# A decoder step on one core: the crossed plain products of three chunks left out, VectorE writing their result across the partition halves, and the first round slots laid out anew

## The reference

```python
def step(S, inp):
    r_t, w_t, k_t, v_t, kk_t, b_t = inp
    sk = jnp.einsum('bhvk,bhk->bhv', S, kk_t)
    S = S * w_t[:, :, None, :] - sk[..., None] * b_t[:, :, None, :] + v_t[..., None] * k_t[:, :, None, :]
    return S, jnp.einsum('bhvk,bhk->bhv', S, r_t)

def _layer(x, pos, s_wkv, s_ret, s_shift, p):
    h = _rmsnorm(x, p['norm_mix_pre'])
    z = h @ p['w_in']
    ya, s_wkv, s_shift = _rwkv7_branch(za, s_wkv, s_shift, ...)
    yb, s_ret = _retention_branch(zb, pos, s_ret, p['gn_b_gain'], p['gn_b_bias'])
    m = jax.nn.sigmoid(ga) * (ya @ p['w_out_a']) + jax.nn.sigmoid(gb) * (yb @ p['w_out_b'])
    x = x + _rmsnorm(m @ p['w_o'], p['norm_mix_post'])
    f = (jax.nn.silu(h @ p['w_ffn_gate']) * (h @ p['w_ffn_up'])) @ p['w_ffn_down']
```

## Time and profile before

| | |
|---|---|
| median of 3 runs | 1286.19 us (1283.54 to 1286.68) |
| the profiled execution | 1286.61 us |
| its span, first to last instruction | 1284.4 us |
| mean granted TensorE clock | 0.988 |
| the rounds of layer 0 | 109.45 to 160.76 us |
| the rounds of layer 1 | 740.29 to 792.47 us |

### The profile page before, as it was taken

One profiled execution on the slowest core, in us unless ns is written; L12 is line 12 of the kernel. 1 busy time (PEld: TensorE's weight loads), 2 busy tenths in 40 slices (PEclk: granted clock), 3 DMA queues, 4 the chain that ended last, 5 costly groups with the idle time before them and its releaser, 6 DMA issues.

```text
span 1284.4 us, 27898 instructions
## 1 busy us (share of the span) xinstructions
PE 1223.7 (95%) x12056; PEld 1159.6 (90%) x12056; DVE 859.4 (67%) x1476; ACT 558.1 (43%) x849; POOL 141.3 (11%) x160
## 2 busy tenths in 40 slices
PE   6999899999998999999999998999999989999996
PEld 5999787998998999999898987889889989999996
DVE  4887558888776666653388954688878566666433
ACT  4553345444435433344454544355453453333432
POOL 0004463100000000000000071900100000000000
PEclk9999999999998999999999999999999989999998
DMA  6433134644453545444434424264354435444441
GB/s 212 143 117 117 53 120 152 228 135 145 139 165 115 185 140 159 148 147 150 147 98 131 123 80 110 87 224 148 131 173 126 155 97 164 148 148 149 148 149 71
DMA packets 51177, 179.12 MB, mean 139 GB/s; under 512 B 6256, under 2 KB 7024, under 8 KB 49776
## 3 DMA queue, kind: packets, MB, share of 16 engines
q1 hardware_dynamic: 42576, 153.77, 38.1%
q10 hardware_dynamic: 8480, 23.58, 5.3%
HBM read 166.18 MB, written 8.53 MB: 136 GB/s over the span
## 4 chain that ended last, share of the span: by engine, by line
PE 82%; DVE 10%; ACT 4%; issue 3%; DMA 1%; ACTq 0%; SPq 0%; DVEq 0%
PE dense L1362 51%; PE core L1362 31%; DVE w_lo L890 3%; ACT w_hi L591 2%; DVE x L939 1%; DVE y_out L937 1%; DMA ret_s<-ret_t 1%; DVE ret_t L1288 1%; ACT L579 0%; DMA x<-x_t 0%; DVE bonus L1008 0%; DVE tmp L994 0%; ACT sq_pair L811 0%; DVE bonus L1004 0%; DVE s_ga L1160 0%
## 5 line engine op out<-in xcount | busy, mean ns | idle before, releaser
L890 DVE TENSOR_TENSOR w_lo<-w_raw,w_hi 128x1024 fp32r<-128x1024 f32 x282 | 352.8, 1253 | 222.0 <-ACT w_hi L591 220.8
L591 ACT ACTIVATE w_hi<-w_raw 128x1024 fp32r<-128x1024 f32 x282 | 297.8, 1057 | 446.6 <-PE dense L1362 300.0
L1362 PE MATMUL dense<-h_hi,w_hi 128*128 128x320 f32 x1296 | 416.8, 322 | 22.9 <-DVE h_lo L894 11.4
L1362 PE MATMUL dense<-h_lo,w_hi 128*128 128x320 f32 x1296 | 404.1, 312 | 0.0
L1362 PE MATMUL dense<-h_hi,w_lo 128*128 128x320 f32 x1296 | 404.0, 312 | 0.0
L1362 PEld LDWEIGHTS dense<-h_hi,w_hi 128*128 128x128 f32 x1296 | 246.9, 190 | 43.0 <-issue 35.0
L1362 PEld LDWEIGHTS dense<-h_lo,w_hi 128*128 128x128 f32 x1296 | 247.1, 191 | 1.4 <-issue 0.2
L1362 PEld LDWEIGHTS dense<-h_hi,w_lo 128*128 128x128 f32 x1296 | 246.7, 190 | 0.0
L1362 PE MATMUL core<-h_hi,w_hi 128*128 128x320 f32 x416 | 129.3, 311 | 0.0
L1362 PE MATMUL core<-h_hi,w_lo 128*128 128x320 f32 x416 | 128.9, 310 | 0.0
L1362 PE MATMUL core<-h_lo,w_hi 128*128 128x320 f32 x416 | 128.9, 310 | 0.0
(11 more groups left out here) (299 smaller groups left out, 1982.6 us busy)
## 6 DMA issues: line engine op xcount, KB each, us to landing
w_raw<-wts SPq DMA_DIRECT2D x282, 512.0 KB, 3.5
ret_t<-ret_t ACTq DMA_DIRECT2D x16, 256.0 KB, 3.7
ret_s<-ret_t ACTq DMA_DIRECT2D x16, 256.0 KB, 2.4
ret_rest<-ret_d ACTq DMA_DIRECT2D x2, 1536.0 KB, 8.6
qk_rot<-qk_raw SPq DMA_DIRECT2D x8, 320.0 KB, 6.2
dmask<-rconst ACTq DMA_DIRECT2D x2, 1152.0 KB, 5.6
s_st<-wkv_st ACTq DMA_DIRECT2D x2, 1024.0 KB, 5.0
wkv_s<-s_st ACTq DMA_DIRECT2D x2, 1024.0 KB, 4.2
```

The costliest lines, as they stand in the source:

```text
L591: act.activation(w_hi[n % RING][:, :], w_raw[n % RING][:, :], ACT.Copy).then_inc(hi_ready.sem, 1)
L890: dve.tensor_tensor(w_lo[r][:, :], w_raw[r][:, :], w_hi[r][:, :].bitcast(F32), ALU.subtract).then_inc(low_made.sem, 1)
L1362: return pe.matmul(out, lhsT, rhs, start=start, stop=stop)
```

## The change

Four things change, in both layers:

1. The jobs `mx1`, `mx2`, `mx3` are gone. For chunks 1 to 3, ACT copies the plain product into `m_sq` as before, and DVE then reads the same bank and writes the masked beginning of `x_sq` to the other half of the partitions, by two operations on 64 partitions each. It waits for the job and for ACT's copy first.
2. PE frees such a bank only when both have been there.
3. The first twelve slots become eleven, with `vt0`, `vt1` and `vt2` among them; slots 13 to 48 become 12 to 47, with `e14` and `d33` alone in theirs.
4. PIECE_AT, LOW_AT and MASKS follow. The pieces have the same sizes; POOL takes the four `xt` first, then the four `x`, and the levels' masks of chunk 0 after those of chunks 1 to 3.

```diff
-ROUNDS = ("vt0", "mt0 mx1", "mt1 mx2", "mt2 mx3", "mt3 kt0", "m0 kt1", "m1 kt2", "m2 kt3", "m3 e01", "mt4 e02", "e00 e03",
-          "m4 kt4", "tb0 dt01", "d01 tk0", "dt00 dt02", "d00 dt03", "d02 e11", "d03 tk1", "e10 e12", "e04 dt11", "dt10 e13",
+ROUNDS = ("mt1 kt0", "mt2 kt1", "mt3 kt2", "mt0 kt3", "m1 vt0", "m2 vt1", "m3 e01", "m0 e02", "mt4 e03", "e00 kt4",
+          "m4 vt2", "tb0 dt01", "d01 tk0", "dt00 dt02", "d00 dt03", "d02 e11", "d03 tk1", "e10 e12", "e04 dt11", "dt10 e13",
           "d10 dt12", "d11 tk2", "d12 dt13", "d13 e21", "e20 e22", "dt04 tk3", "d04 e23", "dt20 dt21", "d20 dt22", "d21 dt23",
-          "d22 tk4", "d23 e31", "e30 e32", "e14 vt1", "dt30 e33", "d30 dt31", "d31 dt32", "d32 dt33", "d33 vt2", "e40 e41",
+          "d22 tk4", "d23 e31", "e30 e32", "e14", "dt30 e33", "d30 dt31", "d31 dt32", "d32 dt33", "d33", "e40 e41",
           "dt14 e42", "tb1 vt3", "dt40 e43", "tb2 dt41", "tb3 dt42", "tb4 vt4", "dt43")
-PIECE_AT = {at: (n // 3, THIRDS[n % 3]) for n, at in enumerate((2, 5, 8, 12, 16, 20, 24, 28, 32, 37, 42, 48))}
-LOW_AT = {10: 1, 18: 2, 30: 3, 42: 4}
+PIECE_AT = {at: (n // 3, THIRDS[n % 3]) for n, at in enumerate((2, 5, 8, 11, 15, 19, 23, 27, 31, 36, 41, 47))}
+LOW_AT = {9: 1, 17: 2, 29: 3, 41: 4}
-MASKS = ("xt0", "x1", "xt1", "x2", "xt2", "x3", "xt3", "x0", "p10", "p20", "p11", "p21", "p12", "p22", "p13", "p23", "xt4", "x4",
+MASKS = ("xt1", "xt2", "xt3", "xt0", "x1", "x2", "x3", "x0", "p11", "p21", "p12", "p22", "p13", "p23", "p10", "p20", "xt4", "x4",
-PARTS = {"mt": ("xt", "mrb"), "m": ("x", "m"), "mx": ("x",)}
-V_OPS = [(part, lv, s) for name, lv, s in JOBS if not on_act((name, lv, s)) for part in PARTS.get(name, (name,))]
+PARTS = {"mt": ("xt", "mrb"), "m": ("x", "m")}
+def parts_of(job):
+    if on_act(job):
+        return ("x",) if job[0] == "m" else ()
+    return PARTS.get(job[0], (job[0],))
+V_OPS = [(part, job[1], job[2]) for job in JOBS for part in parts_of(job)]
...
-                    elif name in ("m", "mx"):
+                    elif name == "m" and s in FLIP:
+                        dve.wait_ge(*round_a(layer, A_AT[job]))
+                        for half in range(2):
+                            here, there = slice(C * half, C * half + C), slice(C - C * half, 2 * C - C * half)
+                            ins = dve.tensor_tensor(pairs(x_sq, s, C)[there], p64[here], mask(M_X1)[here], ALU.mult)
+                        ins.then_inc(round_v.sem, 1)
+                    elif name == "m":
                         masked(x_sq, p64, M_X1)
-                        if name == "m":
-                            masked(m_sq, p64, kind(s, M_STR))
+                        masked(m_sq, p64, kind(s, M_STR))
...
-                            need(emptied(layer, JOBS[n - ROUND_BANKS]))
+                            freed = JOBS[n - ROUND_BANKS]
+                            need(emptied(layer, freed))
+                            if freed[0] == "m" and freed[2] in FLIP:
+                                need(made(layer, ("x", 0, freed[2])))
```

More of the change, by code:

```diff
@@ L1052, in _ @@
                         low(layer, T_V + LOW_AT[i])
-                    if on_act(job):
+                    if not parts_of(job):
                         continue
@@ L1536, in product @@
                         return halves(ps64, b_dec[:, of] if s == HP else b_st[:, b64], i2)
-                    if name in ("m", "mx"):
-                        return (across if name == "mx" else halves)(ps64, ar[:, b128][:, 0:C], b_st[:, b64])
+                    if name == "m":
+                        return halves(ps64, ar[:, b128][:, 0:C], b_st[:, b64])
                     if name == "e":
```

## The result

The changed kernel took 1286.80 us (median of 20 runs, 1283.05 to 1290.70), the kernel before 1283.58 us (20 runs beside it, 1280.09 to 1289.71). The ratio is **1.0023, with a 95% interval of 1.0013 to 1.0034**. It is slower, by an amount inside the 0.3% that I had called the same; I had forecast 0.28% less, so the sign is wrong.

A forecast was written before the change was run, and what follows sets the result against it. PE bounds the kernel: matmul time in the rounds' first twelve slots, instruction count in the other 36. Gains of 1.1 and 0.7 make 1.8 us a layer, 3.6 for both, so 1282.6 us (0.28% less); range 1279.4 to 1287.0.

The forecast's parts named there:

- the first half's gain: First twelve slots of the rounds' stage, eleven after: 1.67 + 0.60 - 1.05 = 1.2 us less a layer, 1.1 kept.
- POOL's longer row, put at no cost: POOL's adds on `x` start some 4 us later; its mask for slot 19 counted hidden by 0.6 us, no cost.
- the second half's 0.7: Other 36 slots of the rounds' stage: 96 fewer PE instructions, 0.7 us less a layer, between nothing and 1.5.
- the stage behind, put at nothing: Stage after the rounds: shifted instruction boundaries may remove or make a stop; counted nothing, 0.5 us a layer either way.
- The new waits: First slots, PE waiting for DVE or ACT: 0.3 ahead of slot 10, 0.55 for `w_lo`, 0.2 in slot 8; 1.05 us.
- The 0.55 for `w_lo`: PE waiting for DVE's `w_lo` before the fourth piece, wanted at 122.06 and ready at 122.6: 0.55 us.
- The wait of 0.60: After old slot 10, PE idle until ACT copies chunk 3's plain product; forecast to go, 0.60 us less a layer.
- removed work: PE, first slots: three jobs of 32 instructions gone, 7.57 us of slots against 9.24, 1.67 us less a layer.
- my 0.85 for a pair: DVE's two operations on 64 partitions after each plain product: 0.85 us a pair, some 1.5 us more on DVE.
- The slow rival: DVE's writes to the other half of the partitions are dear, 1.2 us each: 1292.0 us in all, chance 0.07.
- only the first half gains: Rival: stops not from instruction count, or DVE's steps replace them; 1.1 us a layer, 2.2, 1284.0 us, chance 0.23.
- The range: Whole kernel's time: 1279.4 to 1287.0 us, leaving out the slow rival and the upper end of the fast one.

The follow-up runs named there:

- e11: Changed kernel with the two half-partition products written to their own half, so no crossing write (part of the result left wrong): 1.0022 of the kernel before.
- e6: The changed kernel once more, unchanged: 1289.48 us, 1.0050 of the kernel before.
- e1: Changed kernel with the stage's third `w_lo` moved from ahead of slot 29 to ahead of slot 34: 1.0001 of the kernel before.
- e3: Changed kernel with POOL's last four masks (chunk 3 and 4's `kt`) held until `e14` of slot 34 is done: 1.0005 of the kernel before.
- e7: Changed kernel with POOL waiting, ahead of its mask for `p43`, until the third `w_lo` has been made: 1283.04 us, 1.0001 of the kernel before.
- e10: Changed kernel with POOL waiting, ahead of its mask for `p41`, for `dt20` of slot 28 on PE: 1.0009 of the kernel before.
- e14: Repeat of e7, the changed kernel with POOL's wait for `w_lo` ahead of `p43`: 1.0002 of the kernel before.
- e2: Changed kernel with the stage's third `w_lo` one slot later, ahead of slot 30, still inside POOL's row of masks: 1.0009 of the kernel before.
- e9: No kernel computation: 147 trials of `w_lo` early or late in POOL mask rows, up to 26 long; the 61 long ones ended 1.08 or 1.09 us behind their row.
- e4: Kernel before with only the stage's third `w_lo` moved from ahead of slot 30 to ahead of slot 29: 0.9995 of the kernel before.
- e15: Kernel before with POOL waiting for `e10` of slot 19 ahead of `kt0`'s masks, which gives a longer row: 1.0006 of the kernel before.

## Why the prediction was wrong, step by step

In short: the first half's gain was right. POOL's longer row, put at no cost, cost 2.6 to 2.9 us a layer; the second half's 0.7 did not come; and the stage behind, put at nothing, lost some 2 us. As an estimate for the changed kernel, from the averages given below: 2.8 us gained in the two first halves, against 5.9 for the holds, 0.9 in the second halves and 2.2 behind them, so 6.2 slower. The two sets of runs gave 3.2 and 6.1.

**The first half: right, and a little better.** I had 1.1 us gained; it is 1.41 in each layer. The new waits, which I had at 1.05 us, are 0.32 and 0.23, PE's loads ahead of slots 8 and 10:

```profile
117.61 0.17 PEld L1376 LDWEIGHTS core<-b_st,ar 64*64 64x64 f32 x2 [0.32 <-issue]
...
120.42 0.17 PEld L1376 LDWEIGHTS core<-xt,m_sq 64*64 64x64 f32 x2 [0.23 <-DVE m_sq L1071]
...
117.49 1.75 DVE L1079 TENSOR_TENSOR x_sq<-core,mk 64x256 f32<-64x256 f32 x4 [1.13 <-PE core L1376]
...
120.60 1.31 DVE L899 TENSOR_TENSOR w_lo<-w_raw,w_hi 128x1024 fp32r<-128x1024 f32 x1
```

The matmuls of slot 8 name ACT's `m_sq` as their releaser. The 0.55 for `w_lo` ahead of the fourth piece did not come: it began ahead of POOL's row and took 1.31, not 1.74. The wait of 0.60 is gone, and no later one took its place in this half. The sum itself was not exact: with waits of 0.55 in place of 1.05 it would have given 1.6, and PE's busy time fell by 1.26 (15.54 to 14.28), not by 1.67. Waits counted too long and removed work counted too large made up for each other in part. Four half-partition products in a row took 1.75, so 0.44 each where full ones follow at 0.33; my 0.85 for a pair stands (0.86). The Trainium skill ("VectorE: DVE Perf Modes", Two Vector instructions with no wait between them) has the instruction held when the start quadrant changes: with these 0.44 the trace agrees. The slow rival, dear crossing, is excluded by e11.

**POOL: the step that failed.** The cost of POOL's later masks, "hidden by 0.6 us, at no cost", was read from POOL's own consumer alone, and for that it was right: PE did not wait for chunk 4's `xt`. But POOL's masks start 2 us later (120.79 against 118.72), and PE's rounds come 1.4 us earlier, so the pauses of 1.59 and 0.30 us, in which POOL had waited for PE, are gone. By the time `w_lo` comes, the row without a pause is 15 and 17 masks long in the two layers, where it was 6 and 7, and past some 13 `w_lo` no longer gets its turn. Price: six stages with a long hold (the changed kernel, e6, e11) last 53.2 us on average, the ten of e1, e3, e7, e10 and e14 last 50.3. That is **2.9 us a layer**, 5.9 in all. With the two of e2, also held, of 53.13 and 50.58 us, it is 2.6 a layer; single stages spread by several us, and that of 50.58 is no longer than one without a hold. The times bear the size out: e7 is 3.8 us under the first median of the changed kernel and 6.4 under the one taken beside it. I had even shown a `w_lo` of 1.74 us beside POOL, and took that as the worst that the two do to each other.

The Trainium skill ("SBUF — State Buffer", Who interferes with whom) has VectorE and GpSimd exclude each other when a VectorE instruction has two inputs in SBUF and the GpSimd one reads SBUF; issue order decides which of them waits. With the 0.41 us beside PSUM and the 1.72 us masks the trace agrees. For a long row it does not: up to 13 masks that began after `w_lo` went ahead of it in e9.

**The second half: the other step that failed.** I had it 0.7 us shorter, for the 96 instructions (only 64 of them fall into this half: 2405 records before, 2341 now). In the ten stages without a long hold it lasts 35.8 us on average (34.4 to 36.8), where the four of the kernel before have 35.3 (34.6 to 36.3). So no gain shows, and a loss of 0.45 lies within the spread. What is in its place is seen in part. PE stops at its blocks as before, only at other slots, such as these of e14 and of e7:

```profile
145.03 0.21 PE L1378 MATMUL dense<-xt,p_sq 64*64 64x64 f32 x1 [0.68 <-issue]
149.88 0.27 PE L1378 MATMUL core<-e_sq,x_sq 64*64 64x64 f32 x2 [0.70 <-issue]
```
```profile
152.25 0.41 PE L1378 MATMUL dense<-h_hi,w_hi 128*128 128x320 f32 x1 [1.10 <-issue]
```

I added up PE's gaps of over 0.35 us, from one matmul's start to the next, that end 1.1 to 1.55 us behind the landing of a packet of its program. In layer 0 they are 4.6 to 7.0 us in e1, e3, e7, e10 and e14, and 3.3 to 4.8 in the kernel before (twice) and e4; in layer 1 there is no such difference (3.5 to 5.3 against 4.0 to 6.7), and in e15, the old order too, layer 0 has 1.3. A faster first half may leave the blocks less time to arrive, so that the second pays for it, but these sums are too scattered to show it, and no run was made to isolate it. The cause of the missing 0.7 stays open. Whole stage: 51.25 us before (four stages), 50.29 without the hold, so 0.96 a layer where I had 1.8.

**The stage behind it: a cost that I had put at nothing.** Between 168 and 314 us (two starts of `w_hi`) each of the ten profiles of the changed order takes 1.6 to 4.1 us longer than the mean of three of the old order (the kernel before twice, e4), which differ by 0.5; for the changed kernel, e6 and e11 it is 2.2 on average. But e15, the old order with one wait more on POOL, takes 2.3 longer as well, so it is not the new order alone that can do this. Part is PE's clock. PE waits for DVE's `ret_t` for 1.47 to 2.00 us at 272 to 276 us in all ten profiles of the changed order, for 0.61 in all four of the old, and behind this wait or one at 299 the clock fell in six of the ten, in one of the four (e15, behind a wait of 2.11 us). e1 and the kernel before, PE there, and e1's clock in the 4 us that follow:

```profile
272.83 1.19 PE L1376 MATMUL core<-qk_rot 64*128 64x256 f32 x12 [1.51 <-DVE ret_t L1302]
...
274.00:278.00 4.00, 4.00 (x27) 2.54 (x26) 2.24 (x8) 0.00 (x0) 0.00 (x0) 0.57 0.76 264
```
```profile
272.50 1.19 PE L1362 MATMUL core<-qk_rot 64*128 64x256 f32 x12 [0.61 <-DVE ret_t L1288]
```

Why PE reaches that place in another phase was not tried. With this, the 0.96 a layer are used up, and e1, e3, e7, e10 and e14 lie between 1.0001 and 1.0009 with 1.0 in every interval. So the rival "only the first half gains" was the nearest of those that I wrote down, and it too lacked POOL's row.

**The range** (1279.4 to 1287.0) held the 1286.8, by 0.2 us, and that is luck. It was built on a kernel before of 1286.19 us, which took 1283.58 beside the changed one. Its upper end lies 0.8 us above the kernel before that it was built on, and the measured difference is 3.2.

## What to carry to other kernels

Where VectorE and GpSimd both work from SBUF, a pause of GpSimd is worth something: count how many of its instructions run without one ahead of each long VectorE instruction, not only whether GpSimd is in time for its own consumers. A faster first half can take such pauses away. One wait put into GpSimd's stream, for the VectorE instruction itself, gave back 3.8 to 6.4 us here.

And don't add the gain of removed instructions in a second stretch to that of the first unless a run shows both: here the first half kept its 1.41 us, and the second gave nothing. That the arrival of the program is what took it is argued, not shown.

## What was not expected of the hardware

- `w_lo` (1.2 us alone) beside a row of GpSimd masks of 0.69 us each: through behind the running mask in 76 of 76 trials with up to 12 masks begun without a pause, held to the end of the row in 45 of 45 with 16 or more, 16 of 26 between. The longest was 10.1 us in e9 and 8.4 us in the kernel. A pause of 1.17 us ahead was enough to restart the count (e10). Why the count (or the time since the pause) matters no run shows.
- The crossing write from PSUM to the other half of the partitions costs nothing: 0.42 us for 64x256 either way.
- Around waits of 3.29 and 1.87 us of PE ahead of slot 32 the granted clock falls to the lower level; to the end of the stage it is 0.90 and 0.82 on average.
